# A memory tile multiplied ahead of the modulation: its load, its norm and its two halves moved to the program's first instructions

## The chip, the cores and the metric

The kernel runs on one core of one Trainium2 chip. A time is the device time of one execution in microseconds (us). Three executions of the kernel before gave 1676.72, 1678.35 and 1678.55 us, median 1678.35. One more execution was profiled; all rows below are from it. Engines: PE multiplies matrices, DVE, ACT and POOL do the element-wise work, and SP's queue issues nearly all of the transfers.

## The reference, cut to what matters

256 tokens of width 1024 go through two blocks. The first mixes the tokens (attention with 8 heads, mLSTM with 4) and then sends them through 32 experts; the second is a GLA layer and an S5 layer, which both attend to a memory of 256 rows.

```python
mod = jax.nn.silu(c) @ w_ada[l] + b_ada[l]                 # 6 x 1024 numbers: the modulation
sh1, sc1, g1, sh2, sc2, g2 = jnp.split(mod, 6, axis=-1)
h = modulate(x, norm1_g[l], sh1, sc1)                      # rms_norm(x) * (1 + sc1) + sh1
proj = h @ w_in[l]
# ... attention, mLSTM, w_out, router, experts ...
mem_n = rms_norm_2(mem, mem_norm_w)                        # second block, but it needs only mem
k, v = jnp.split(mem_n @ w_kv, 2, axis=-1)                 # w_kv[0]: 1024 x 2048
```

The product `mem_n @ w_kv[0]` depends on nothing that the first block computes. The kernel therefore places its four tiles among the first block's work.

## The kernel before, in words

All arithmetic is float32. The weights come as tiles of 2 MB (128 partitions x 4096 numbers, which is 1024 rows by 512 columns). They go through a ring of three slots, in the order that the tuple `FRONT` gives; tile n goes to slot n modulo 3, and its load waits until PE has finished tile n-3. `tile(n)` in SP's program does this: it waits on `tile_done` and issues the load.

The names of tiles: A0 to A11 are the modulation (`w_ada`). `ada_tile` (L278) multiplies one of them by the vector silu(c), which is short work: 16 instructions of PE. ACT copies the result (`take_part`, L565), and then `ada_columns` (L290, piece C) or `ada_row` (L300, piece G) turns it into the layout wanted, and DVE adds the bias. A0 to A3 give shift and scale of the first norm, without which the input of all further multiplications, `hT`, cannot be made. Q, K, V, U0, U1, VM, OM are `w_in`, O0 and O1 are `w_out`, and M0 to M3 are the four quarters of `w_kv[0]`: M0 and M1 make the keys `kmT`, M2 and M3 the values `vm`. A tile of `w_in` or of `w_kv` is multiplied in two halves (`half_tile`, L259 for kind "tm", L264 for kind "fm"; M00 is the first half of M0).

Stage `stage_mix` begins the program. Its order is written out by hand, engine by engine, and semaphores join the engines. PE does A0, C0, A1, C1, A2, the transposes of the scaled x (`turn`, L186), C2, A3, C3. DVE then makes `hT` (L701), PE the gates (L408), and Q, K, V and the rest follow without a break. The memory is loaded behind tile Q (L381). Its squares on ACT (L590), its scaling on DVE (L751), its transposes on PE (`turn` between K0 and K1) and its multiplication by the norm's weights on DVE (L754, result `memT`) lie beside Q, K and V. M00 and M01 stand beside the mLSTM's steps, between A7 and A8.

`stage_route` follows. PE does M1 (L972), transposes the normed x, does A10, M20, the router's logits (L983), G10, transposes back (L989), M21, A11, M30, the five ranking multiplications (L996 to L1000), G11 and M31. Beside them DVE picks the experts: it finishes `chosen` (L1093), which the ranking waits for, and after the ranking it makes `rank`, the last third of `h2` (L1127) and the last row of the modulation (L1041). SP loads A10, M2, the first expert's six half tiles, A11, M3, one row, and the second expert's six half tiles as the ring's slots come free. A stage ends when every engine is done, and `stage_experts` begins.

PE's results of pieces go to two banks in turn. The string given to `TwoBanks` names the pieces in order and the engine that empties each; a piece waits until the piece two places before it has been taken.

## Time and profile before

| | |
|---|---|
| three executions, median | 1678.35 us |
| the profiled execution | 1676.78 us |
| its span, first to last instruction | 1675.0 us |
| PE busy in the span | 1566.1 us, 93% |
| mean granted clock of PE | 0.982 of full |
| start of PE's first multiplication | 12.53 us |
| start of the gates' multiplications | 36.81 us |
| start of the first Q half | 41.92 us |
| `stage_route`, PE's first to last instruction | 228.4 to 284.8 us |
| first instruction of `stage_experts` on DVE | 287.18 us |

The share of PE over the whole span says that PE is nearly always at work. It does not say where it is not: the gaps lie in the first 37 us, at the ends of stages and in a few waits later. The change touches the first 37 us, two halves in the middle of `stage_mix`, and the end of `stage_route`. So the profile is read there: which wait ends last before each step of PE.

In a row of the timeline the first number is the start, the second the time that the group spans, then engine, line, operation, result and operands, count, and in brackets the idle time before it and what ended it. One multiplication in the program is two instructions in the trace (x16 for the 8 of an `ada_tile`, x32 for the 16 of an "fm" half).

### The profile page before, as it was taken

How to read it: one execution, taken by the hardware profiler on the slowest of the kernel's cores; microseconds unless marked ns; L12 is line 12 of the kernel's file. 1: busy time of each engine (PE TensorE's matmuls, PEld its weight loads, DVE VectorE, ACT ScalarE, POOL GpSimd, SP SyncE). 2: the span in 40 equal slices, each digit the busy share in tenths (PEclk: the TensorE clock that was granted, in tenths of full speed). 3: DMA queues.
4: the chain of work that ended last, by engine and by line, in shares of the span. 5: the costliest groups of instructions: out<-in, count | busy, mean ns of one | idle time of the engine just before them, and what ended most of it. 6: DMA issues, size and time to landing. Idle time of an engine off the chain costs nothing. (4 is left out here: it accounts for less than half of the span.)

```text
span 1675.0 us, 20622 instructions
## 1 busy us (share of the span) xinstructions
PE 1566.1 (93%) x8428; PEld 917.0 (55%) x8428; DVE 578.7 (35%) x958; ACT 321.9 (19%) x547; POOL 54.0 (3%) x125
## 2 busy tenths in 40 slices
PE   5999998999999999994999999988999899699997
PEld 2485654444344444442445887547777775388843
DVE  2445323111111111113202111215999999720000
ACT  2222101111111111111200201003333343230000
POOL 0000000000000000000000000001111111000000
PEclk8999999999999999997999999998999999799999
DMA  9444647899999999993232242342333333124330
GB/s 402 169 157 188 257 200 318 339 422 422 422 422 422 422 422 422 422 410 130 107 144 101 101 151 101 146 156 94 146 114 113 115 148 129 63 101 151 151 151 25
DMA packets 46024, 371.59 MB, mean 222 GB/s; under 512 B 5888, under 2 KB 10368, under 8 KB 11408
## 3 DMA queue, kind: packets, MB, share of 16 engines
q1 hardware_dynamic: 45824, 369.75, 55.0%
q10 hardware_dynamic: 144, 1.05, 0.2%
q8 instruction: 40, 0.66, 0.2%
q14 instruction: 16, 0.13, 0.0%
HBM read 369.73 MB, written 1.05 MB: 221 GB/s over the span
## 5 line engine op out<-in xcount | busy, mean ns | idle before, releaser
L1228 PE MATMUL ps<-ring,x_gathered 128*64 128x512 f32 x1024 | 225.2, 592 | 0.9 <-DVE x_gathered L1296 0.9
L1911 PE MATMUL ps<-hT,ring 128*128 128x256 f32 x768 | 174.7, 386 | 1.9 <-PEq L113 1.9
L1416 PE MATMUL ps<-ring,zT 128*128 128x512 f32 x384 | 165.5, 592 | 0.0
L1911 PEld LDWEIGHTS ps<-hT,ring 128*128 128x128 f32 x768 | 146.0, 192 | 29.9 <-issue 10.4
L1228 PEld LDWEIGHTS ps<-ring,x_gathered 128*64 128x64 f32 x1024 | 73.6, 137 | 146.6 <-issue 146.6
L1305 DVE TENSOR_TENSOR act_slots<-gate,ps 64x512 f32<-64x512 f32 x32 | 22.1, 690 | 378.6 <-ACT gate L1267 378.6
L1416 PEld LDWEIGHTS ps<-ring,zT 128*128 128x128 f32 x384 | 72.9, 190 | 90.1 <-issue 89.9
L1251 PE MATMUL ps<-ring,act_turned 128*64 128x512 f32 x512 | 116.9, 598 | 0.0
L1529 PE MATMUL ps<-hT,ring 128*128 128x256 f32 x512 | 111.9, 380 | 0.0
L2086 PE MATMUL ps<-uT,ring 128*128 128x256 f32 x512 | 111.0, 379 | 0.0
L1529 PEld LDWEIGHTS ps<-hT,ring 128*128 128x128 f32 x512 | 96.8, 190 | 16.0 <-issue 3.1
L2086 PEld LDWEIGHTS ps<-uT,ring 128*128 128x128 f32 x512 | 97.2, 190 | 13.2
L1524 PE MATMUL ps<-ring,hT 128*128 128x512 f32 x192 | 83.7, 594 | 2.4 <-PEq L113 2.4
L1203 PE MATMUL ps<-y,selT 64*128 64x512 f32 x272 | 77.9, 641 | 4.2 <-DVEq L1290 3.5
L1251 PEld LDWEIGHTS ps<-ring,act_turned 128*64 128x64 f32 x512 | 33.9, 136 | 79.1 <-issue 54.8
L259 PE MATMUL ps<-ring,hT 128*128 128x512 f32 x160 | 69.8, 593 | 0.0
L1192 PEld LDWEIGHTS ps<-sel,h 128*128 128x128 bf16 x1584 | 48.7, 99 | 27.5 <-issue 27.5
L1524 PEld LDWEIGHTS ps<-ring,hT 128*128 128x128 f32 x192 | 36.0, 190 | 47.0 <-issue 47.0
L1267 ACT ACTIVATE gate<-ps 64x512 f32<-64x512 f32 x32 | 18.9, 591 | 188.1 <-PE ps L1228 188.1
L1192 PE MATMUL ps<-sel,h 128*128 128x64 bf16 x1584 | 52.6, 194 | 0.0
L259 PEld LDWEIGHTS ps<-ring,hT 128*128 128x128 f32 x160 | 29.9, 190 | 35.8 <-issue 35.8
L1934 PE MATMUL ps<-s_x_re,c_bar 128*32 128x256 f32 x128 | 11.1, 418 | 38.4 <-issue 35.4
(446 smaller groups left out, 1676.9 us busy)
## 6 DMA issues: line engine op xcount, KB each, us to landing
ring<-in_experts SPq DMA_DIRECT2D x192, 1024.0 KB, 15.8
ring<-in_weights SPq DMA_DIRECT2D x75, 2048.0 KB, 7.5
b_raw<-in_s_b SPq DMA_DIRECT2D x16, 128.0 KB, 7.4
c_raw<-in_s_c SPq DMA_DIRECT2D x16, 128.0 KB, 7.2
x<-in_x ACTq DMA_DIRECT2D x1, 1024.0 KB, 5.3
mix_room<-in_mem SPq DMA_DIRECT2D x1, 1024.0 KB, 17.2
rows_b_g<-in_rows SPq DMA_DIRECT2D x1, 1024.0 KB, 19.3
out<-x SPq DMA_DIRECT2D x2, 512.0 KB, 2.7
```

The costliest lines, as they stand in the source:

```text
L259: last = pe.matmul(bank, src[:, kk, h * P:(h + 1) * P], w[:, kk, :], start=(kk == 0), stop=(kk == KD - 1))
L1192: last = pe.matmul(xg_ps[:, f, :], a["h2"][:, t, part, f * P:(f + 1) * P], sel[:, t, :], start=(t == 0 and part == 0), stop=(t == TT - 1 a ...
L1203: last = pe.matmul(acc[:, t, n, :], selT[rows, b, t * P:(t + 1) * P], y[rows, :], start=start, stop=stop, skip_group_check=True)
L1228: last = pe.matmul(h_ps[rows, :], xg[:, f, :], w[:, kk, m, :], start=(f == 0), stop=(f == KD - 1))
L1251: last = pe.matmul(y_ps[rows, :], act_t[:, f, :], w[:, kk, n * 512:(n + 1) * 512], start=(f == 0), stop=(f == 3))
L1267: act.activation(gate[:], h_ps[lower, :], ACT.Silu).then_inc(silu_done, 1)
L1305: dve.tensor_tensor(act_s[:], gate[:], h_ps[upper, :], ALU.mult).then_inc(act_ready, 1)
L1416: last = pe.matmul(self.bank(n, t), self.zT[:, 8 * kb + kk, t * P:(t + 1) * P], w[:, kk, :], start=(first and kk == 0), stop=(self.ends(i) ...
L1524: last = pe.matmul(bank, k.hT[:, kk, h * P:(h + 1) * P], w[:, kk, :], start=(kk == 0), stop=(kk == KD - 1))
L1529: last = pe.matmul(bank[:, f, :], w[:, kk, (2 * h + f) * P:(2 * h + f + 1) * P], k.hT[:, kk, :], start=(kk == 0), stop=(kk == KD - 1))
L1911: last = pe.matmul(out[:, f, :], w[:, kk, (2 * h + f) * P:(2 * h + f + 1) * P], rhs[:, kk, :], start=(kk == 0), stop=(kk == KD - 1))
L2086: last = pe.matmul(o[:, f, :], w[:, kk, f * P:(f + 1) * P], uT[:, 8 * r + kk, :], start=(r == 0 and kk == 0 and f % 2 == 0), stop=(r == 1 ...
```

## The change

The tile M0 leaves `FRONT` and stands as one more tile at the end of the weights (index `T_END`). The memory and this tile are now loaded ahead of the ring's first three tiles; the tile goes in two halves to two buffers, `qk` and `mix`, that are not yet in use. ACT squares the memory before x, DVE scales the memory before x, and PE begins with the memory's transposes. DVE then makes `memT`, PE multiplies M00, then A0, then M01, and goes on with C0 as before. In the middle of the stage, where M00 and M01 were, M20 and M21 stand now, as kind "tm", with their results to `vm`. In `stage_route` M3 takes the places that M2 had, and the two places of M3 (beside A11 and after the ranking) are gone, with one load of 2 MB less.

```diff
-FRONT = (..., "A6", "A7", "M0", "A8", "A9",
-         "O0", "O1", "M1", "A10", "M2", "A11", "M3")
+FRONT = (..., "A6", "A7", "M2", "A8", "A9",
+         "O0", "O1", "M1", "A10", "M3", "A11")
...
@@ stage_mix, sync
                 sp.dma_start(k.const[:], d["consts"]).then_inc(small_in, 16)
+                sp.dma_start(mem, d["mem"]).then_inc(mem_in, 16)
+                for i in range(2):
+                    sp.dma_start(first_w[i], d["weights"][T_END][:, i * 2048:(i + 1) * 2048]).then_inc(first_in, 16)
                 for n in range(RING):
                     tile(n)
...
                 tile(4)
-                sp.dma_start(mem, d["mem"]).then_inc(mem_in, 16)
...
@@ stage_mix, tensor
+                def first_half(h):
+                    p = f"M0{h}"
+                    out = banks.bank(p).rearrange("p (f t) -> p f t", f=2)
+                    for f in range(2):
+                        for kk in range(KD):
+                            w = first_w[kk // 4].rearrange("p (k n) -> p k n", k=4)[:, kk % 4, (2 * h + f) * P:(2 * h + f + 1) * P]
+                            last = pe.matmul(out[:, f, :], w, k.memT[:, kk, :], start=(kk == 0), stop=(kk == KD - 1))
+                    last.then_inc(banks.done(p), 1)
+                pe.wait_ge(mem_scaled, TT)
+                turn(k, pe, memn, KD, fm(0, 4), mem_turned)
+                pe.wait_ge(memT_ready, 1)
+                pe.wait_ge(first_in, 32)
+                first_half(0)
                 pe.wait_ge(crep_ready, 1)
-                for m in range(3):
-                    ada_tile(k, banks, pe, m, crep)
-                    if m < 2:
-                        ada_columns(k, banks, pe, m, part)
+                ada_tile(k, banks, pe, 0, crep)
+                pe.wait_ge(*banks.free("M01"))
+                first_half(1)
+                ada_columns(k, banks, pe, 0, part)
+                ada_tile(k, banks, pe, 1, crep)
+                ada_columns(k, banks, pe, 1, part)
+                ada_tile(k, banks, pe, 2, crep)
...
                 half("K0")
-                pe.wait_ge(mem_scaled, TT)
-                turn(k, pe, memn, KD, fm(0, 4), mem_turned)
                 half("K1")
...
-                half("M00", "fm", k.memT)
+                half("M20", "tm", k.memT)
...
-                half("M01", "fm", k.memT)
+                half("M21", "tm", k.memT)
...
@@ stage_mix, scalar: the memory's squares stand before x's
-                for m in range(4):
+                take_fm("M00", a["kmT"][:, 0:2, :])
+                take_part(0)
+                take_fm("M01", a["kmT"][:, 2:4, :])
+                for m in range(1, 4):
                     take_part(m)
...
@@ stage_mix, vector
                 dve.tensor_copy(crep[:], bc(csil[:], 2, 32)).then_inc(crep_ready, 1)
+                dve.wait_ge(mem_rstd_ready, 1)
+                for t in range(TT):
+                    dve.tensor_scalar(memn[:, t, :], mem[:, t, :], rstd_m[:, t:t + 1], None, ALU.mult).then_inc(mem_scaled, 1)
+                ...
+                dve.wait_ge(mem_turned, KD)
+                for f in range(KD):
+                    last = dve.tensor_scalar(k.memT[:, f, :], fm(0, 4)[:, f, :], k.col("mem_norm_w", f), None, ALU.mult)
+                last.then_inc(memT_ready, 1)
                 take_columns(0, 0)
...
@@ stage_route, tensor
-                half_tile(k, banks, pe, "M20", "tm", k.memT)
+                half_tile(k, banks, pe, "M30", "tm", k.memT)
...
-                half_tile(k, banks, pe, "M21", "tm", k.memT)
+                half_tile(k, banks, pe, "M31", "tm", k.memT)
                 ada_tile(k, banks, pe, 11, a["crep"])
-                half_tile(k, banks, pe, "M30", "tm", k.memT)
                 pe.wait_ge(chosen_ready, 1)
...
                 ada_row(k, banks, pe, 11, a["part"])
-                half_tile(k, banks, pe, "M31", "tm", k.memT)
```

PE's order at the program's start, before (L278 is an A tile, L290 a C piece, L186 the transposes of x, L408 the gates):

```order
L278 MATMUL ps<-ring,crep 32x512 x8
L290 MATMUL ps<-const,ada_part 128x1 x4
L278 MATMUL ps<-ring,crep 32x512 x8
L290 MATMUL ps<-const,ada_part 128x1 x4
L278 MATMUL ps<-ring,crep 32x512 x8
L186 MATMUL ps<-const,mix_room 128x128 x16
L290 MATMUL ps<-const,ada_part 128x1 x4
L278 MATMUL ps<-ring,crep 32x512 x8
L290 MATMUL ps<-const,ada_part 128x1 x4
L408 MATMUL ps<-hT,w_gate 4x256 x16
```

The same place in the changed kernel (the first L186 transposes the memory, L405 is M00 and, after the first A tile, M01):

```order
L186 MATMUL ps<-const,mix_room 128x128 x16
L405 MATMUL ps<-memT,qk 128x256 x4
L405 MATMUL ps<-memT,mix 128x256 x4
L405 MATMUL ps<-memT,qk 128x256 x4
L405 MATMUL ps<-memT,mix 128x256 x4
L278 MATMUL ps<-ring,crep 32x512 x8
L405 MATMUL ps<-memT,qk 128x256 x4
L405 MATMUL ps<-memT,mix 128x256 x4
L405 MATMUL ps<-memT,qk 128x256 x4
L405 MATMUL ps<-memT,mix 128x256 x4
L290 MATMUL ps<-const,ada_part 128x1 x4
L278 MATMUL ps<-ring,crep 32x512 x8
```

The memory's transposes and one half stand ahead of the first A tile, the other half behind it; from the C piece on the order is the old one.

PE at the end of `stage_route`, before (L259 are the halves, L278 is A11, L996 and the four below it the ranking, L300 G11):

```order
L259 MATMUL ps<-ring,memT 128x512 x8
L278 MATMUL ps<-ring,crep 32x512 x8
L259 MATMUL ps<-ring,memT 128x512 x8
L996 MATMUL ps<-chosen,const 128x32
L997 MATMUL ps<-chosen,const 128x32
L998 MATMUL ps<-chosen,const 128x32
L999 MATMUL ps<-chosen,const 128x32
L1000 MATMUL ps<-chosen,const 128x32
L300 MATMUL ps<-ada_part,const 128x512
L259 MATMUL ps<-ring,memT 128x512 x8
```

And the same place in the changed kernel:

```order
L259 MATMUL ps<-ring,memT 128x512 x8
L278 MATMUL ps<-ring,crep 32x512 x8
L1017 MATMUL ps<-chosen,const 128x32
L1018 MATMUL ps<-chosen,const 128x32
L1019 MATMUL ps<-chosen,const 128x32
L1020 MATMUL ps<-chosen,const 128x32
L1021 MATMUL ps<-chosen,const 128x32
L300 MATMUL ps<-ada_part,const 128x512
```

The half between A11 and the ranking and the half behind G11 are gone.

## Rows read from the trace of the kernel before

**Rows 1.** The page, part 1: busy time, share of the span, instructions.
```profile
PE 1566.1 (93%) x8428; PEld 917.0 (55%) x8428; DVE 578.7 (35%) x958; ACT 321.9 (19%) x547; POOL 54.0 (3%) x125
```

**Rows 2.** Stretches: length, busy (instructions) of PE, PEld, DVE, ACT, POOL, clock, DMA share, GB/s.
```profile
12.50:36.80 24.30, 16.82 (x112) 8.15 (x112) 8.39 (x28) 5.36 (x8) 0.00 (x0) 0.86 1.01 425
...
41.90:194.60 152.70, 152.59 (x692) 95.89 (x690) 69.30 (x141) 36.02 (x78) 4.33 (x5) 1.00 0.47 184
```

**Rows 3.** SP's timeline: issue of the ring's first three tiles; their time to landing.
```profile
1.64 1.68 SPq L370 DMA_DIRECT2D ring<-in_weights  x3
...
DMA to landing us min/median/max: 10.8/15.2/19.4
```

**Rows 4.** Timeline of the first 60 us, all engines.
```profile
7.65 1.04 ACT L572 ACTIVATE mix_room<-x 128x1024 f32<-128x1024 f32 x1
...
10.24 0.71 POOL L179 TENSOR_TENSOR x_rstd<-x_rstd,const 128x2 f32<-128x2 f32 x1
...
12.53 3.64 PE L278 MATMUL ps<-ring,crep 128*32 128x512 f32 x16 [12.53 <-DMA ring<-in_weights]
...
18.05 1.41 DVE L681 TENSOR_SCALAR mix_room<-x,x_rstd 128x1024 f32<-128x1024 f32 x2
...
20.51 1.05 PE L290 MATMUL ps<-const,ada_part 128*128 128x1 f32 x8 [0.72 <-ACT ada_part L565]
...
28.81 1.92 PE L278 MATMUL ps<-ring,crep 128*32 128x512 f32 x16 [0.32 <-DMA ring<-in_weights]
...
31.45 1.05 PE L290 MATMUL ps<-const,ada_part 128*128 128x1 f32 x8 [0.72 <-ACT ada_part L565]
...
33.04 3.71 DVE L701 TENSOR_SCALAR hT<-ps,mod 128x256 f32<-128x256 f32 x8
...
36.81 5.19 PE L408 MATMUL ps<-hT,w_gate 128*4 128x256 f32 x32 [4.30 <-DVE hT L701]
...
41.92 18.29 PE L259 MATMUL ps<-ring,hT 128*128 128x512 f32 x42
```

**Rows 5.** Stretches of 1 us in the gates' multiplications, columns as in rows 2.
```profile
37.00:38.00 1.00, 1.00 (x6) 0.28 (x4) 0.00 (x0) 0.00 (x0) 0.00 (x0) 0.50 0.96 410
...
40.00:41.00 1.00, 1.00 (x12) 0.40 (x10) 0.00 (x0) 0.00 (x0) 0.00 (x0) 0.99 1.00 426
```

**Rows 6.** PE's timeline later in `stage_mix`.
```profile
62.63 1.91 PE L186 MATMUL ps<-const,mix_room 128*128 128x128 f32 x16
...
168.57 1.92 PE L278 MATMUL ps<-ring,crep 128*32 128x512 f32 x16
170.42 7.17 PE L264 MATMUL ps<-memT,ring 128*128 128x256 f32 x32
```

**Rows 7.** Timelines of PE, then DVE and ACT, at the end of `stage_route`.
```profile
266.08 1.92 PE L278 MATMUL ps<-ring,crep 128*32 128x512 f32 x16
268.83 7.13 PE L259 MATMUL ps<-ring,memT 128*128 128x512 f32 x16 [0.83 <-DMA ring<-in_weights]
...
277.78 7.03 PE L259 MATMUL ps<-ring,memT 128*128 128x512 f32 x16
...
261.82 0.23 DVE L1093 TENSOR_TENSOR chosen<-is_first,is_second 128x64 f32<-128x64 f32 x1
...
277.04 0.23 DVE L1114 SCALAR_TENSOR_TENSOR rank<-ps,chosen 128x64 f32<-128x64 f32 x1 [10.28 <-PE ps L1000]
...
280.42 0.68 DVE L1041 TENSOR_TENSOR rows_b_g<-ps,rows_b_g 128x512 f32<-128x512 f32 x1
287.18 0.48 DVE L1288 MEMSET y<- 128x512 f32 x1 [6.08 <-issue]
...
284.84 0.60 ACT L1016 ACTIVATE vm<-ps 128x512 f32<-128x512 f32 x1 [8.24 <-PE ps L259]
```

**Rows 8.** SP's timeline and time to landing: A11 and M3; then A11 alone.
```profile
242.47 3.96 SPq L947 DMA_DIRECT2D ring<-in_weights  x2
...
DMA to landing us min/median/max: 21.4/21.4/21.4
```

More of the change, by code:

```diff
@@ L329, in stage_mix @@
         memn, mem = tokens(r3), tokens(r4)
+        first_w = [x[:].rearrange("p t n -> p (t n)") for x in (qk, mix)]
         scores, pT = (r[:].rearrange("p (b h t q) -> p b h t q", b=2, h=2, t=TT) for r in (r3, r4))
@@ L336, in stage_mix @@
         ig, fg = gate_rows[:, 0, :], gate_rows[:, 1, :]
-        banks = TwoBanks(k, "mix", "A0:act C0:dve A1:act C1:dve A2:act C2:dve A3:act C3:dve GT:dve Q0:act Q1:act K0:act K1:act "
+        banks = TwoBanks(k, "mix", "M00:act A0:act M01:act C0:dve A1:act C1:dve A2:act C2:dve A3:act C3:dve GT:dve Q0:act Q1:act K0:act K1:act "
                          "V0:act V1:act U00:act U01:act U10:act A4:act U11:act G4:dve VM0:act A5:act VM1:act G5:dve "
-                         "OM0:act OM1:act A6:act C6:dve A7:act M00:act C7:dve M01:act A8:act C8:dve A9:act C9:dve")
-        names = ("small_in", "mix_const_in", "pos_in", "rows_in", "x_in", "mem_in", "w_gate_in", "cexp_ready", "crep_ready",
+                         "OM0:act OM1:act A6:act C6:dve A7:act M20:act C7:dve M21:act A8:act C8:dve A9:act C9:dve")
+        names = ("small_in", "first_tile_in", "mix_const_in", "pos_in", "rows_in", "x_in", "mem_in", "w_gate_in", "cexp_ready", "crep_ready",
                  "x_summed", "x_rstd_ready", "x_scaled", "x_turned", "hT_ready",
@@ L587, in _ @@
                 act.activation(q4[96:100, 0:P], b[:, 0:P], ACT.Exp, bias=sc[:, 2:3]).then_inc(e_ready, 1)
-                act.wait_ge(mem_in, 16)
-                for t in range(TT):
-                    act.activation(memn[:, t, :], mem[:, t, :], ACT.Square, accum_out=ss_m[:, t:t + 1]).then_inc(mem_summed, 1)
                 take("Q1", qk[:, 1, 0:512])
@@ L637, in _ @@
                 take_part(7)
-                take_fm("M00", a["kmT"][:, 0:2, :])
-                take_fm("M01", a["kmT"][:, 2:4, :])
+                take("M20", a["vm"][:, 0, 0:512])
+                take("M21", a["vm"][:, 1, 0:512])
                 take_part(8)
@@ L677, in _ @@
                 dve.tensor_copy(crep[:], bc(csil[:], 2, 32)).then_inc(crep_ready, 1)
-                take_columns(0, 0)
+                dve.wait_ge(mem_rstd_ready, 1)
+                for t in range(TT):
+                    dve.tensor_scalar(memn[:, t, :], mem[:, t, :], rstd_m[:, t:t + 1], None, ALU.mult).then_inc(mem_scaled, 1)
                 dve.wait_ge(x_rstd_ready, 1)
@@ L747, in _ @@
                 dve.tensor_copy(q4[0:4, :], b).then_inc(m_ready, 1)
-                dve.wait_ge(mem_rstd_ready, 1)
-                for t in range(TT):
-                    dve.tensor_scalar(memn[:, t, :], mem[:, t, :], rstd_m[:, t:t + 1], None, ALU.mult).then_inc(mem_scaled, 1)
-                dve.wait_ge(mem_turned, KD)
-                for f in range(KD):
-                    last = dve.tensor_scalar(k.memT[:, f, :], fm(0, 4)[:, f, :], k.col("mem_norm_w", f), None, ALU.mult)
-                last.then_inc(memT_ready, 1)
                 dve.wait_ge(quads_ready, 1)
@@ L936, in stage_route @@
         tps = k.ps[:, 0:4, :].rearrange("p b (f t) -> p (b f) t", f=2)
-        banks = TwoBanks(k, "route", "M10:act M11:act A10:act M20:act G10:dve M21:act A11:act M30:act G11:dve M31:act")
+        banks = TwoBanks(k, "route", "M10:act M11:act A10:act M30:act G10:dve M31:act A11:act G11:dve")
         names = ("router_in", "norm_f_in", "x1_summed", "x1_rstd_ready", "x1_scaled", "x1_turned", "h_ready", "logits_done",
@@ L952, in _ @@
                 tile(TILE_OF["A10"])
-                tile(TILE_OF["M2"])
+                tile(TILE_OF["M3"])
                 for j in range(RING):
@@ L956, in _ @@
                 tile(TILE_OF["A11"])
-                tile(TILE_OF["M3"])
                 at = ROWS["norm_f_g"][0]
@@ L1022, in _ @@
                 take("A10", a["part"][:])
-                take("M20", a["vm"][:, 0, 0:512])
+                take("M30", a["vm"][:, 0, 512:1024])
                 act.wait_ge(h_turned, 1)
@@ L1028, in _ @@
                 act.activation(dl[:], dl[:], ACT.Exp).then_inc(exp_done, 1)
-                take("M21", a["vm"][:, 1, 0:512])
+                take("M31", a["vm"][:, 1, 512:1024])
                 act.wait_ge(rest_ready, 1)
@@ L1033, in _ @@
                 take("A11", a["part"][:])
-                take("M30", a["vm"][:, 0, 512:1024])
-                take("M31", a["vm"][:, 1, 512:1024])
             @block.vector
@@ L2298 @@
         wide(g["s5_w_in_2"][0]), kv[1], wide(g["s5_w_glu_2"][0]),
-        in_order(wide(g["w_out_2"][1]), "s5"),
+        in_order(wide(g["w_out_2"][1]), "s5"), front["M0"][None],
     ]
@@ L2302 @@
     weights = np.concatenate(groups, axis=0)
[L2303 removed]
+    assert weights.shape[0] == T_END + 1
     def by_feature(v, n):
```

13 lines of the change are left out of this document (7 added, 6 removed).

## The prediction

> **What bounds the kernel now.** I read the shares of busy time first, then the timeline around each place that the change touches, then the transfers there. PE is busy for 93% of the span [rows 1], so work on PE that is removed is worth its time, and so is work that moves into a gap. After the first Q half PE does not stop for the rest of `stage_mix`: 152.59 of 152.70 us [rows 2]. There every microsecond of work is a microsecond of time. The first 37 us are different. From 12.5 to 36.8 us PE is busy for 16.82 of 24.30 us while the transfers run at 425 GB/s with a share of 1.01 [rows 2]: the queue is full, and PE waits for tiles (the bracket of the row at 28.81 names the DMA) [rows 4]. In `stage_route` the end is set by PE's last half at 277.78 and ACT's copy of it, which ends at 284.84 + 0.60 = 285.44; DVE is done at 280.42 + 0.68 = 281.1 [rows 7].
>
> So the question is one of two places: what the front of the program pays for M0, and what the router's end gives back. The middle is an exchange.
>
> **The front, step by step.** The change puts 3 MB (memory 1 MB, tile 2 MB) ahead of A0, and 16 transposes, 7 us of multiplication and a DVE step ahead of A0 on PE.
>
> First the transfers. The ring's first three tiles are issued from 1.64 us on, the third at about 2.8, and land 10.8 to 19.4 us after issue, so at 12.4 and 22.2 us: 4.9 us for each 2 MB [rows 3]. A0's own 4.9 us begin at 7.5. The memory, in that place now, lands after 2.45 us, at 10.0; M0 at 14.9; A0, A1 and A2 7.35 us later than before, at about 19.8, 24.7 and 29.6.
>
> Now PE's chain, which starts with the memory:
> - ACT squares the memory from 10.0 on. For x the squares began at 7.65 and POOL's rstd ended at 10.24 + 0.71 = 10.95, together 3.30 us [rows 4]. That gives 13.3.
> - DVE scales two halves: 1.41 us [rows 4], 14.75.
> - PE's 16 transposes take 1.91 us at full clock [rows 6]. PE has done nothing before. Before the change its first tile, A0, took 3.64 us where later ones take 1.92, a factor of 1.9 [rows 4, 6]. So 3.6 us: 18.4.
> - DVE makes `memT` from PSUM by 8 instructions like those of `hT`: 3.71 us plus 0.05 [rows 4], 22.15. PE stands still meanwhile; x's squares and scaling (another 3.3 + 1.4 us behind the memory's) fit in.
> - M00 takes 7.0 us from its start to the next piece's at full clock (7.17 with its end) [rows 6]. [...] Some 3.3 to 3.6 us at half speed lose 1.7 to 1.8 us; I take 1.9, because the work before the pause is short. 31.05.
> - A0 1.9 (landed since 19.8) and M01 7.0: 39.95. C0 0.9: 40.85. ACT's copies of M00, of A0's result and of M01 (0.60 each) lie beside PE's next piece.
> - A1 1.9, then 0.72 of waiting for ACT's copy [rows 4], C1 0.95, A2 1.9: 46.3. No wait for a tile any more.
> - x's transposes 1.8, C2 0.9, A3 1.9: 50.9. A3's load is issued when A0 is done (32.9) into an empty queue; even with the 19.4 us of rows 3, which were those of a full one, it would come at 52.3, and with their shortest, 10.8, at 43.7, before PE wants it at 49.0. K, V and Q follow A1, A2, A3 in the same way; Q is issued at 42.8 and wanted at 62.
> - From A3's end to the gates' start: 36.81 - 30.73 = 6.1 us, the copy, C3, DVE's column and `hT` [rows 4]. The gates start at 57.0.
>
> Before, they started at 36.81 [rows 4]. The front grows by 20.2 us. The transfers alone would have moved it by 7.35. The difference is the step that decides: once PE's chain begins at 14.75, it has 42 us of work and hand-offs in a row, and it is later than every tile. The gap that M0 was to fill was not there at the time at which `memT` can be there.
>
> [...]
>
> **The middle.** The memory's transposes between K0 and K1 go: 1.91 us with its end, 1.8 from start to start [rows 6]. DVE loses the scaling and `memT` there and ACT two squares, on engines that PE does not wait for. M20 and M21 replace M00 and M01: a "tm" half takes 7.03 us, an "fm" half 7.17 [rows 6, 7], so -0.1 at most. Their copies are of equal size, and the load stands in the same place of the ring.
>
> **The router's end.** M30 and M31 take the places of M20 and M21, at equal cost. Two halves go from PE. A11 runs at 266.08 as before, since its load is at the same place of the queue: issued at 242.47, landed at 263.9 [rows 8]. It ends at 268.0. `chosen` has been ready since 262.05 [rows 7], so the ranking follows at once. It took from 275.9 (268.83 + 7.0) to DVE's start at 277.04, so 1.15 us: DVE starts at 269.15. DVE then needs 281.1 - 277.04 = 4.06 us: 273.2. G11 needs ACT's copy of A11, at about 269.1 behind the copy of `h2`, and is done at 270.2, in DVE's shadow. The stage now ends with DVE at 273.2, not with ACT at 285.44: -12.2 us. The two halves are worth 14.06 and the 0.83 us wait for M3's load goes too [rows 7], but DVE's tail, once covered by M31, is 3 us long behind PE and now stands free. SP's wait for the last row and the second expert's loads are earlier than this, with 2 MB less in the queue.
>
> The experts, GLA and S5 are unchanged but for the tiles' slots in the ring.
>
> **The sum.** +20.2 - 1.8 - 0.1 - 12.2 = +6.1 us. Against the profiled execution, 1676.8, that is 1682.9; this execution lay 1.6 us below the median of the three, and against that median it is 1684.4. I say 1684.
>
> **The bounds of what no row shows.** [...] The memory's transposes: at full clock -1.7. The memory's landing: at the earliest 9.5, or 2.5 us later if its packets share the queue with M0's. The clock of the later short pieces: A1 to A3 could lose up to 1.7 us once, as A0 did. The experts' start: PE stands still for some 6 us where it was 3.5, and may lose up to 1.7 us more, or nothing. Together 1680.7 to 1691, most of it in 1681.5 to 1687.5.
>
> **The rivals.** A measurement of this kernel tells 0.2% (3.4 us) from no change, so "same" is 1675.0 to 1681.7.
>
> 1. Faster: the transfers set the front, as now. Then only 7.35 us are added there and the total is 1678.35 + 7.35 - 1.8 - 0.1 - 12.2 = 1671.6. For it: the queue's share of 1.01 and PE's 7.5 idle us of 24.3 [rows 2]. Against it: those idle us are spread over hand-offs of 0.7 us and waits between tiles, and M00 cannot start before `memT`, at 22.15, where A0 lands at 19.8. The point from which it decides: the front may grow by 14.1 us at most; my chain would have to be 6 us too long. 9%.
> 2. No change that can be measured: PE runs at full clock in the memory's transposes and M00, -3.6, so 1680.8, and some hand-off is shorter. 13%.
> 3. [...] 10%.
> 4. The router's end gives less: A11's load shares the queue with the second expert's first load, which is now issued when A10 is done (about 246) and not at 266, and lands as late as M3 did, 268.8. Then A11 is 2.7 us later and the total 1687.1. Against it: A11 is issued first. 8%.
>
> My forecast has 60%. It and rivals 3 and 4 are slower by over 0.2%: 78%. Same 13%, faster 9%. The range has to leave out no more than 2 in 10: from 1678 (rival 1 out, rival 2 in) to 1689 (rival 3's end out).
>
> **What would show each step.** The gates' first multiplication starts near 57 us, and its shift from 36.81 is the front's cost; M00 starts near 22 behind DVE's `memT` and takes 8 to 9.5 us; A1, A2, A3 start without a wait for a DMA; the first Q half starts near 62. The end of `stage_route`, from M1's first multiplication to DVE's first instruction of the experts, is 58.8 us before (228.38 to 287.18) and should be 46.6. I am wrong if PE waits for the ring's tiles in the front, if M00 starts before 20 us, or if the router's stage gives back 14 us or more.

## The result, and the profile after

The changed kernel takes 1687.74 us (median of 7 runs, 1685.55 to 1691.43); the kernel before took 1680.97 us in the 7 runs beside it (1676.72 to 1683.32). The ratio is 1.0044, with a 95% interval from 1.0029 to 1.0058: slower by 0.3 to 0.6%. The forecast was 1684.0 us in a range of 1678 to 1689, slower with a chance of 78%. Against the median that it started from (1678.35) it was a growth of 5.7 us; measured was one of 6.8. The starting point had been low, though: in these runs the kernel before lies 2.6 us above 1678.35, so the growth was forecast within 1.1 us and the absolute time only within 3.7, near the top of the range.

The profiled execution of the changed kernel was its slowest: 1691.43 us with a span of 1689.7, against 1676.78 and 1675.0. These 14.7 us are more than the medians differ, so a second profile of the same kernel was taken (e1 below, span 1683.4). Where the two disagree, both are told.

The page's first part. PE's busy time grew by 10.7 us [rows 1], although the number of its instructions did not: 8428 in both.

```profile
PE 1576.8 (93%) x8428; PEld 925.1 (55%) x8428; DVE 578.7 (34%) x958; ACT 321.7 (19%) x547; POOL 54.4 (3%) x125
```

The timeline of the front, PE's rows with the DVE and ACT rows that release them:

```profile
10.00 1.06 ACT L592 ACTIVATE mix_room<-mix_room 128x1024 f32<-128x1024 f32 x1 [2.29 <-DMA mix_room<-in_mem]
...
14.83 3.68 PE L186 MATMUL ps<-const,mix_room 128*128 128x128 f32 x16 [14.83 <-DVE mix_room L703]
...
18.54 3.23 DVE L709 TENSOR_SCALAR memT<-ps,cols 128x256 f32<-128x256 f32 x8 [1.43 <-PE ps L186]
...
21.82 3.78 PE L405 MATMUL ps<-memT,qk 128*128 128x256 f32 x8 [3.32 <-DVE memT L709]
...
25.40 2.77 PE L405 MATMUL ps<-memT,mix 128*128 128x256 f32 x8
...
28.01 1.89 PE L405 MATMUL ps<-memT,qk 128*128 128x256 f32 x8
...
31.55 1.92 PE L278 MATMUL ps<-ring,crep 128*32 128x512 f32 x16
...
41.36 1.92 PE L278 MATMUL ps<-ring,crep 128*32 128x512 f32 x16
...
44.98 1.92 PE L278 MATMUL ps<-ring,crep 128*32 128x512 f32 x16
...
49.51 1.92 PE L278 MATMUL ps<-ring,crep 128*32 128x512 f32 x16
52.15 1.05 PE L290 MATMUL ps<-const,ada_part 128*128 128x1 f32 x8 [0.72 <-ACT ada_part L585]
57.50 5.48 PE L431 MATMUL ps<-hT,w_gate 128*4 128x256 f32 x32 [4.30 <-DVE hT L731]
```

The chain runs as it was written down beforehand: memory at 10.0, transposes from 14.8, `memT`, M00 at 21.8, A0, M01, the other modulation tiles. The four rows of L278 are A0 to A3, and none has a DMA in its bracket; before, A3's had one, of 0.32 us [rows 4]. PE no longer waits for tiles in the front, it is itself late. The clock shows in durations: the same 16 transposes took 1.91 us in the old place [rows 6] and take 3.68 here; M00's four quarters (8 instructions each) take 3.78, 2.77, 1.89 and 1.89. The views' own clock column says 1.00 for the whole of this trace from 12 to 54 us, also in the row below, where PE had only 5 instructions; in e1's row of the same stretch, where the column says 0.50, it had 6. So the front is read by durations here:

```profile
22.00:24.00 2.00, 2.00 (x5) 1.64 (x6) 0.00 (x0) 0.00 (x0) 0.00 (x0) 1.00 1.02 434
```

The gates start at 57.50, 20.7 us later than before [rows 4].

The end of `stage_route`, PE's rows, then DVE's, which answer to rows 7:

```profile
273.34 4.13 PE L1005 MATMUL ps<-w_router,hT 128*128 128x36 f32 x32
277.27 2.05 PE L300 MATMUL ps<-ada_part,const 128*128 128x512 f32 x2
279.12 3.62 PE L1011 MATMUL ps<-const,hT 128*128 128x128 f32 x16
282.53 7.36 PE L259 MATMUL ps<-ring,memT 128*128 128x512 f32 x16
289.81 1.92 PE L278 MATMUL ps<-ring,crep 128*32 128x512 f32 x16
...
292.58 0.39 PE L1021 MATMUL ps<-chosen,const 128*128 128x32 f32 x2
```
```profile
293.01 0.23 DVE L1132 SCALAR_TENSOR_TENSOR rank<-ps,chosen 128x64 f32<-128x64 f32 x1 [4.13 <-PE ps L1021]
...
296.39 0.68 DVE L1059 TENSOR_TENSOR rows_b_g<-ps,rows_b_g 128x512 f32<-128x512 f32 x1
298.44 0.48 DVE L1306 MEMSET y<- 128x512 f32 x1 [1.38 <-issue]
```

The last row, DVE's first instruction of the experts, came at 287.18 before and comes at 298.44. Between A11's multiplications and the ranking there is no half any more, and DVE's row with `rows_b_g` is now the last thing the stage waits for. But the router's own pieces are slow here. The stretches (columns as in rows 2) name the reason:

```profile
276.00:278.00 2.00, 2.00 (x10) 1.75 (x10) 0.41 (x2) 0.00 (x0) 0.00 (x0) 0.59 1.06 442
278.00:280.00 2.00, 2.00 (x7) 1.11 (x6) 1.65 (x13) 0.00 (x0) 0.00 (x0) 0.50 1.05 434
280.00:282.00 2.00, 2.00 (x11) 2.00 (x10) 1.54 (x13) 0.00 (x0) 0.00 (x0) 0.50 0.97 412
282.00:284.00 2.00, 2.00 (x7) 1.25 (x6) 1.43 (x6) 1.23 (x1) 0.00 (x0) 0.71 0.96 395
```

PE was busy all through, 2.00 of 2.00 us in each row, and the clock fell late in the 36-column multiplications (L1005), which start at 273.34 and take 4.13 us: it is 1.00 from 275 to 276 us and 0.67 from 276 to 277. In the profile shown of before, where the same multiplications start at 252.94 and take 3.66 us, it is 1.00 from 250 to 264 us.

The forecast had named no third place, but there is one: the first 16 instructions of the GLA multiplications, behind the experts' end. They took 7.11 us before. PE's row in the changed kernel, and a stretch in it:

```profile
794.28 8.80 PE L1542 MATMUL ps<-ring,hT 128*128 128x512 f32 x16 [2.38 <-PEq L113]
```
```profile
796.00:798.00 2.00, 2.00 (x4) 0.85 (x3) 0.00 (x0) 0.00 (x0) 0.00 (x0) 0.50 0.77 256
```

### The profile page after: what moved, and what is told of

It reads as the page before. It is cut to its first block and busy times, and to the rows that moved or that the text cites. A ratio compares the mean times of both kernels' runs of the same rounds, so it can differ in the third digit from the quotient of the medians.

```text
span 1689.7 us, 20622 instructions
## 1 busy us (share of the span) xinstructions
PE 1576.8 (93%) x8428; PEld 925.1 (55%) x8428; DVE 578.7 (34%) x958; ACT 321.7 (19%) x547; POOL 54.4 (3%) x125
## 5 line engine op out<-in xcount | busy, mean ns | idle before, releaser
L259 PE MATMUL ps<-ring,hT 128*128 128x512 f32 x160 | 69.6, 593 | 0.0
L259 PEld LDWEIGHTS ps<-ring,hT 128*128 128x128 f32 x160 | 30.0, 190 | 36.3 <-issue 36.3
L1448 DVE TENSOR_TENSOR x<-x,ps 128x512 f32<-128x512 f32 x8 | 5.5, 687 | 120.0 <-PE ps L1434 120.0
## 6 DMA issues: line engine op xcount, KB each, us to landing
mix<-in_weights SPq DMA_DIRECT2D x1, 1024.0 KB, 12.2
```

The lines of the kernel that those rows point to most:

```text
L259: last = pe.matmul(bank, src[:, kk, h * P:(h + 1) * P], w[:, kk, :], start=(kk == 0), stop=(kk == KD - 1))
```

## The experiments

Each kernel's ratio is to the kernel before, run beside it. Five marks, in us, are read from each trace: the start of the gates' multiplications; PE's start on M1 (the M tile in its old place behind O1); the time from there to DVE's first instruction of the experts ("router"); from there to ACT's copy of the last expert's gate ("experts"); and from there to the end of the span ("tail"). M1 and the last three add up to the span.

| kernel | median us (runs) | ratio, 95% | gates | M1 | router | experts | tail |
|---|---|---|---|---|---|---|---|
| before | 1680.97 (7) | | 36.81 | 228.38 | 58.80 | 461.3 | 926.6 |
| changed | 1687.74 (7) | 1.0044, 1.0029 to 1.0058 | 57.50 | 248.78 | 49.66 | 461.6 | 929.6 |
| e1 changed, again | 1685.88 (6) | 1.0037, 1.0023 to 1.0050 | 56.03 | 245.60 | 48.01 | 461.1 | 928.7 |
| e2 without M0 | 1672.22 (5) | 0.9952, 0.9937 to 0.9967 | 36.86 | 228.22 | 46.33 | 462.6 | 930.9 |
| e3 without the tile's load | 1686.39 (5) | 1.0041, 1.0025 to 1.0057 | 56.55 | 246.27 | 48.00 | 461.2 | 928.8 |
| e4 loads alone | 1686.28 (9) | 1.0038, 1.0023 to 1.0053 | 44.37 | 236.59 | 58.66 | 461.2 | 927.2 |
| e5 filled, too long | 1689.70 (6) | 1.0046, 1.0028 to 1.0063 | 58.38 | 249.24 | 46.32 | 462.4 | 930.6 |
| e6 A0 in the first pause | 1684.73 (12) | 1.0022, 1.0011 to 1.0033 | 52.87 | 243.94 | 46.33 | 462.5 | 930.6 |
| e7 M0 in the pause for `hT` | 1680.82 (12) | 1.0002, 0.9989 to 1.0015 | 54.34 | 245.41 | 46.32 | 461.3 | 928.8 |
| e8 that, ranking first | 1677.22 (12) | 0.9973, 0.9961 to 0.9984 | 50.07 | 239.48 | 46.33 | 461.3 | 929.8 |
| e9 before, again | 1676.8 (1) | | 36.88 | 228.45 | 58.66 | 461.2 | 926.7 |
| e10 before, again | 1678.95 (1) | | 36.85 | 229.68 | 59.57 | 461.2 | 926.7 |
| e11 filled, fitting | 1683.17 (12) | 1.0018, 1.0008 to 1.0029 | 53.33 | 244.66 | 46.32 | 462.5 | 930.7 |
| e12 e8 with the old slots | 1675.22 (7) | 0.9967, 0.9955 to 0.9980 | 50.50 | 239.95 | 44.67 | 462.2 | 926.6 |

### e1: the changed kernel again

No edit.

> The changed kernel once more, for a second profile and a second set of times. Theory: the front's cost is a chain on PE that the order fixes, so the gates start at 57.5 us again (within 0.5) and the ratio to before is near 1.0044. The first profile also had 3 us at the low clock between the router's logits and the second M3 half (276 to 283 us). If that stretch belongs to the change, it is there again and M1's start to the experts' first DVE instruction takes 49.7 us. If it was chance, that stretch takes 46.6 us.

The ratio came out as in the first comparison. In this profile the same steps are shorter: transposes 3.40, M00 8.6 us, and the low stretch beside the router costs 1.7 us and not 3.3 (48.01 and 49.66 against the 46.33 us of kernels without one). PE's rows of M00's first two quarters:

```profile
21.46 3.51 PE L405 MATMUL ps<-memT,qk 128*128 128x256 f32 x8 [3.32 <-DVE memT L709]
24.80 1.89 PE L405 MATMUL ps<-memT,mix 128*128 128x256 f32 x8
```

And the clock in it, in the front and beside the router:

```profile
22.00:24.00 2.00, 2.00 (x6) 1.59 (x5) 0.00 (x0) 0.00 (x0) 0.00 (x0) 0.50 1.08 459
24.00:26.00 2.00, 2.00 (x9) 1.69 (x9) 0.00 (x0) 0.00 (x0) 0.00 (x0) 0.86 1.00 426
...
274.00:276.00 2.00, 2.00 (x5) 0.86 (x5) 1.63 (x13) 0.00 (x0) 0.00 (x0) 0.50 1.04 438
276.00:278.00 2.00, 2.00 (x15) 2.00 (x14) 1.56 (x13) 0.00 (x0) 0.00 (x0) 0.71 1.03 434
```

So a single profile of one kernel is not good to better than some 6 us; the stretches at low clock are not equally long in both.

The front differs in one more thing. The transposes took 3.40 us here and not 3.68, because the clock rose before their end: the last two start 0.11 us apart, the first ones 0.21, and an instruction takes 0.27 us at the end and 0.42 before. So, by these durations, the clock rose when PE had done 3 us of transposes and nothing else, and fell again in the pause behind them (0.50 in the row of 22 to 24 us). In the first profile it had not risen by then.

### e2: M0 left out, nothing ahead of A0

```diff
-                sp.dma_start(mem, d["mem"]).then_inc(mem_in, 16)
-                for i in range(2):
-                    sp.dma_start(first_w[i], d["weights"][T_END][:, i * 2048:(i + 1) * 2048]).then_inc(first_in, 16)
...
-                first_half(0)
...
-                first_half(1)
```

The memory's load, norm and transposes are back in their old places.

> The changed kernel with M0 left out altogether: memory loaded, normed and transposed where it was before, no early tile, kmT's first half set to zero (so the keys of half the memory heads are not computed), M2 in the middle and the short router's end kept. Theory: the router's end is worth 12.2 us and the exchange in the middle 0.1, so 12.3 us faster than before (ratio 0.9927) and 19 to 20 us faster than the changed kernel. Rival: the two removed halves are worth their full 14.1 us plus the 0.8 us wait for M3, ratio 0.991. Second rival: the low clock beside the router eats 3 us, ratio 0.9945.

The router's stage took 46.33 us, which puts its gain at 12.5 us. The time, though, did not fall by as much as expected: 0.9952 and not 0.9927. The experts took 462.6 us, 1.3 more than before, and the tail 930.9, 4.3 more. That is where the rest went: the span is 7.0 us shorter. The first is the low clock at the experts' start (0.50 from 272 to 280 us), which the prediction had among its bounds; the second is the first sign that the tail is not untouched.

### e3: the tile's load left out, its multiplications kept

```diff
-        first_w = [x[:].rearrange("p t n -> p (t n)") for x in (qk, mix)]
+        first_w = [x.rearrange("p t n -> p (t n)") for x in (mem, mem)]
...
-                for i in range(2):
-                    sp.dma_start(first_w[i], d["weights"][T_END][:, i * 2048:(i + 1) * 2048]).then_inc(first_in, 16)
```

> The changed kernel without the early load of M0's 2 MB: M00 and M01 are multiplied from the memory's own numbers in its place (the keys of half the memory heads are wrong numbers). All ring tiles land 4.9 us earlier. Theory: PE's chain sets the front, so the gates start at 57.5 us as in the changed kernel and the ratio to before stays 1.0044. Rival: the early loads set the front, then the gates start 4.9 us earlier, at 52.6, and the ratio is 1.0015.

With 2 MB less ahead of A0 the gates start at 56.55, inside the 56.03 to 57.50 of the two profiles with the load, and the ratio is 1.0041 beside 1.0037 and 1.0044, which the intervals do not tell apart. The transfers do not set the changed kernel's front.

### e4: the loads alone

The kernel before, with memory and M0's tile loaded ahead of A0, the tile never used.

```diff
+                sp.dma_start(mem, d["mem"]).then_inc(mem_in, 16)
+                for i in range(2):
+                    sp.dma_start(first_w[i], d["weights"][TILE_OF["M0"]][:, i * 2048:(i + 1) * 2048]).then_inc(first_in, 16)
                 for n in range(RING):
```

> The kernel before with nothing but the two early loads (memory and M0's tile, 3 MB, ahead of A0); M0 stays in the ring and the early copy is not used. All work is where it was. Theory: the front of the kernel before is set by its loads, so everything there moves by 7.35 us: A0 at 19.8, gates at 44.2, and the whole by 7.35 us, ratio 1.0044. Rival: PE's pauses take some of it up, gates before 42 and ratio under 1.003.

PE's rows of A2, A3 and the gates (the view ends within the gates' row; all 32 take 5.58 us):

```profile
29.85 1.92 PE L278 MATMUL ps<-ring,crep 128*32 128x512 f32 x16 [0.69 <-DMA ring<-in_weights]
...
36.38 1.92 PE L278 MATMUL ps<-ring,crep 128*32 128x512 f32 x16 [1.93 <-DMA ring<-in_weights]
...
44.37 1.88 PE L411 MATMUL ps<-hT,w_gate 128*4 128x256 f32 x8 [4.30 <-DVE hT L705]
```

The same 3 MB move this kernel's gates by 7.6 us (7.35 had been worked out), and here the brackets name the DMA. With e3: the front of before is set by the transfers, the changed one by PE's chain.

### e5 and e11: PE kept busy ahead of the transposes and of M00

Needless multiplications before the transposes and behind them: 9 and 7 in e5, 4 and 3 in e11.

```diff
+                pe.wait_ge(small_in, 32)
+                idle_work(4)
                 pe.wait_ge(mem_scaled, TT)
                 turn(k, pe, memn, KD, fm(0, 4), mem_turned)
+                idle_work(3)
                 pe.wait_ge(memT_ready, 1)
```

> The changed kernel with needless multiplications on PE (128x512, into an unused bank): 9 from the constants' landing at 7.5 us to the memory's transposes, 7 in the pause in which DVE makes memT. They delay nothing by more than 0.5 us and keep PE's clock up. Theory: 3.6 to 4.4 us of the front are the low clock in the transposes (3.4 to 3.7 us where 1.9 is full speed) and in M00 (8.7 to 10.3 where 7.0 is), so the gates start at 52.5 to 53.5 and the ratio to before is 1.0015 to 1.002. Rival: the clock is low there for another reason than the pauses, the gates stay at 56 to 57.5 and the ratio at 1.0037 or above.

> As e5, with 4 needless multiplications ahead of the memory's transposes and 3 in the pause for memT, which fit (one takes 0.87 us at full clock and 1.7 us at the low one). Theory: the low clock in the transposes and in M00 costs 3 to 4.5 us of the front, so the gates start at 53 to 54.5 and the ratio to before is 1.0015 to 1.0025. Rival: the filling does not raise the clock in time, the gates stay at 56 or later and the ratio at 1.0035.

In e5 the filling overran: its first 9 ran to 17.8 us and held the transposes up by 2.9 us, its last 7 held M00 up to 25.43. Its time says nothing for either theory, but the transposes took 1.91 us. e11 fits, as PE's rows show:

```profile
7.49 5.65 PE L411 MATMUL ps<-const 128*128 128x512 f32 x8 [7.49 <-DMA const<-in_consts]
14.79 1.97 PE L186 MATMUL ps<-const,mix_room 128*128 128x128 f32 x16 [1.65 <-DVE mix_room L711]
16.59 2.74 PE L411 MATMUL ps<-const 128*128 128x512 f32 x6
20.27 1.99 PE L405 MATMUL ps<-memT,qk 128*128 128x256 f32 x8 [0.93 <-DVE memT L717]
...
53.33 6.52 PE L439 MATMUL ps<-hT,w_gate 128*4 128x256 f32 x32 [4.30 <-DVE hT L739]
```

Transposes and M00 run at full clock; M00 ends at 27.4 and not at 30.1 to 31.6, the gates start 2.7 to 4.2 us earlier than in the two profiles of the changed kernel. The gates' multiplications take 6.52 us here, against 4.92 and 5.48, so a part may be lost again at once (e10, below, shows 6.31 in the kernel before). The ratio is 1.0018. The low clock in transposes and M00 costs 3 to 4 us of front, and even without it the change is slower.

### e6: A0 ahead of M00, in the pause for `memT`

```diff
                 turn(k, pe, memn, KD, fm(0, 4), mem_turned)
+                pe.wait_ge(crep_ready, 1)
+                ada_tile(k, banks, pe, 0, crep)
                 pe.wait_ge(memT_ready, 1)
...
-                ada_tile(k, banks, pe, 0, crep)
+                ada_columns(k, banks, pe, 0, part)
```

> The changed kernel with A0 between the memory's transposes and M00, in PE's pause for memT; M00, C0, M01 follow. A0 lands at 19.8 us. Theory: PE's chain sets the front, so filling 2 to 3 us of the pause brings the gates forward by 1.5 to 3 us, to about 54.5, ratio 1.002 to 1.003. Rival: A0 at the low clock takes 3.6 us and pushes M00 behind memT; nothing is gained, gates at 56.5 or later.

```profile
14.75 3.28 PE L186 MATMUL ps<-const,mix_room 128*128 128x128 f32 x16 [14.75 <-DVE mix_room L703]
19.90 1.92 PE L278 MATMUL ps<-ring,crep 128*32 128x512 f32 x16 [1.88 <-DMA ring<-in_weights]
21.76 1.99 PE L405 MATMUL ps<-memT,qk 128*128 128x256 f32 x8
...
52.87 3.58 PE L431 MATMUL ps<-hT,w_gate 128*4 128x256 f32 x16 [4.30 <-DVE hT L731]
```

PE's rows (the last is cut off by the view's end; all 32 take 6.35 us): A0 lands at 19.90 (19.8 had been worked out) and fits ahead of M00 without moving it. M00 then runs at full clock (1.99 us for its first quarter, and not 3.78 or 3.51): the pause is shorter, 1.88 us and not 3.3. The gates come 3.2 to 4.6 us earlier than in the changed kernel; the ratio is 1.0022.

### e7: M0 in the pause for `hT`

M0's load behind A3's, its halves between C3 and the gates.

```diff
                 tile(3)
+                for i in range(2):
+                    sp.dma_start(first_w[i], d["weights"][T_END][:, i * 2048:(i + 1) * 2048]).then_inc(first_in, 16)
...
                 ada_columns(k, banks, pe, 3, part)
+                pe.wait_ge(first_in, 32)
+                for h in range(2):
+                    pe.wait_ge(*banks.free(f"M0{h}"))
+                    first_half(h)
                 pe.wait_ge(hT_ready, 1)
```

> The changed kernel with M00 and M01 between C3 and the gates, where PE has a pause of 4.3 us for hT, and M0's 2 MB loaded behind A3; memory's load, norm and transposes stay early. Theory: the front then costs 2.5 us (memory ahead of A0), 1.1 us (M00 waits for its tile, at 36.2), 14 us less the pause of 4.3, less 1.7 us because the gates no longer start at the low clock: the first Q half starts at 53.7 and not at 62, the whole is 9 us faster than the changed kernel and 2.3 us faster than before, ratio 0.9986. Rival: a multiplication costs its 14 us wherever it stands in the front, then the first Q half starts at 58 or later and the ratio is 1.001 or above.

The pause of 4.30 us for `hT`, which all kernels above keep, is filled, and the ratio falls from 1.0037 to 1.0002. It is less than expected, for the reason that PE's rows show: another pause of 2.48 us, for M0's own load, and its low clock (0.50 from 38 to 42 us). M00 starts 1.1 us later than expected (37.28 and not 36.2), and the two halves take 17.1 us, 3.1 more than 14.

```profile
37.28 3.78 PE L405 MATMUL ps<-memT,qk 128*128 128x256 f32 x8 [2.48 <-DMA mix<-in_weights]
40.85 3.19 PE L405 MATMUL ps<-memT,mix 128*128 128x256 f32 x8
...
54.34 3.62 PE L431 MATMUL ps<-hT,w_gate 128*4 128x256 f32 x32
57.89 27.73 PE L259 MATMUL ps<-ring,hT 128*128 128x512 f32 x64
```

The first Q half starts at 57.89, where 53.7 was expected. A second stretch of low clock (0.50 from 212 to 214 us), behind a wait of 2.46 us for tile O0 that ended at 211 us, cost another 1.7 us, and the tail was 2.3 us longer than before.

### e8: the tile in two halves, and the ranking ahead of A11

M0 is packed by halves of its columns and each half has its own load and semaphore, so M00 waits for 1 MB only; and PE's five ranking pieces stand ahead of A11, so that DVE's 4 us lie beside A11 and G11.

```diff
-                pe.wait_ge(first_in, 32)
                 for h in range(2):
+                    pe.wait_ge((first_in, second_in)[h], 16)
...
-                ada_tile(k, banks, pe, 11, a["crep"])
                 pe.wait_ge(chosen_ready, 1)
...
                 pe.matmul(k.ps[:, 5, 0:32], k.c("ones"), chosen[:, 1, :], start=False, stop=True).then_inc(ranked, 1)
+                ada_tile(k, banks, pe, 11, a["crep"])
```

> As the kernel before it in this list, and two things more: M0 is packed by halves of its columns, so that M00 needs only the first 1 MB and starts at C3's end (gain 1.1 us), and in the router's stage the five ranking multiplications stand ahead of A11, so that DVE's tail begins 1.9 us earlier and the stage ends at ACT's and G11's pace (gain 1.6 us). Theory: ratio 0.9970, the first Q half at 52.6, M1 to the experts' first DVE instruction 44.7 us. Rival: the router's tail is bound by the copy of h2 on ACT and nothing is gained there, 46.3 us, ratio 0.998.

```profile
31.16 3.31 PE L278 MATMUL ps<-ring,crep 128*32 128x512 f32 x16 [1.17 <-DMA ring<-in_weights]
35.17 1.05 PE L290 MATMUL ps<-const,ada_part 128*128 128x1 f32 x8 [0.70 <-ACT ada_part L585]
36.08 7.15 PE L405 MATMUL ps<-memT,qk 128*128 128x256 f32 x32
43.07 7.07 PE L405 MATMUL ps<-memT,mix 128*128 128x256 f32 x32
50.07 3.62 PE L431 MATMUL ps<-hT,w_gate 128*4 128x256 f32 x32
```

From C3 on PE does not stop, and the gates start 4.3 us earlier than in e7. This version is faster than the kernel before: 0.9973, from 0.9961 to 0.9984. The first Q half comes at 53.63 (52.6 was expected). Its router took 46.33 us with a low clock in it (0.77, 0.50 and 0.88 in the stretches of 2 us from 266 to 272; 44.7 us was expected), e12's 44.67 without (1.00 from 262 to 270), so the ranking's place is worth 1.7 us.

### e9 and e10: the kernel before, twice more

No edit.

> The kernel before once more, for its trace. In the first profile of it the time from the last expert's gate copy to the end is 926.6 us, and the first GLA half takes 7.1 us. In the profiles of kernels with the short router's end it is 928.7 to 930.9, and that half 8.8 to 9.8 us with a low clock. Theory: that is the phase of the clock, which differs from run to run, so here the tail is longer than 926.6, up to 931. Rival: the tail belongs to the change (tiles in other slots of the ring), and is 926.6 to 927.2 here.

> The same once more, for the same question: by the theory the tail lies anywhere from 926.6 to 931, by the rival within 0.6 of 926.9.

Both tails are as in the first profile: 926.7 and 926.7. In e10 the clock fell beside the router in this kernel too (0.84, 0.50 and 0.80 in the stretches of 2 us from 256 to 262, all 1.00 in e9): M1 to the experts took 59.57 us, 0.9 more than in e9. So the low stretch there is not the change's own doing. The gates' multiplications took 6.31 us in e10 and 5.19 in the first profile, with nothing changed.

### e12: e8 with one needless tile behind A11

The tile makes no work but takes a slot, so that all later tiles of the ring lie and are loaded as in the kernel before.

```diff
-         "O0", "O1", "M1", "A10", "M3", "A11")
+         "O0", "O1", "M1", "A10", "M3", "A11", "X")
...
                 tile(TILE_OF["A11"])
+                tile(TILE_OF["X"])
...
+                k.wait_tile(pe, TILE_OF["X"])
+                pe.sem_inc(k.tile_done, 1)
```

> e8 with one needless tile of 2 MB loaded behind A11 in the router's stage and not multiplied, so that every later tile stands in the same slot of the ring as before the change, and the second expert's loads wait as long. From the last expert's gate copy to the end the kernel before takes 926.6 to 926.7 us in three profiles (926.6, 926.6, 926.7) and 927.2 with the early loads alone; e8 takes 929.8, the other kernels with the short router's end 928.7 to 930.9. Theory A: the ring's slots or the loads' order behind them cause it, then the tail is near 926.7 here, and the ratio to before 0.995 to 0.996. Theory B: it is where the steps fall against the clock's changes, which the length of the work ahead decides; then the tail is 928.7 or more and the ratio near 0.9975.

The tail is 926.6 us, the number of the kernel before to a tenth, and PE's row of the first GLA multiplications is back at its old length:

```profile
781.07 7.11 PE L1544 MATMUL ps<-ring,hT 128*128 128x512 f32 x16 [2.37 <-PEq L113]
```

2 MB more are moved, and the span is 3.4 us shorter than e8's (1673.5 against 1676.9): router 1.7 and tail 3.2 us less, experts 0.9 and the part ahead of M1 0.5 more. By the times it is the fastest of those that compute everything, 0.9967, but its interval overlaps that of e8, so that its lead over e8 rests on the two profiles. Against the kernel before it is faster.

## Why the prediction was right, step by step

**The front.** The step that decided was that PE's chain, not the transfers, sets the gates' start. It held: 57.0 us forecast, 57.50 and 56.03 in two profiles, no DMA ahead of A1 to A3. e3 and e4 show it from both sides: without the tile's load the front stays, with the loads alone it moves by 7.6 us. Rival 1 (the transfers set the front) falls with e3.

The single steps up to M00's end were off by at most 0.8 us: the memory's landing 10.0 (10.0), the transposes 14.83 (14.75) for 3.68 and 3.40 (3.6), M00's start 21.82 and 21.46 (22.15; DVE's `memT` took 3.2 and not 3.7 us), M00 9.7 and 8.6 (8.9). That transposes and M00 would run at low clock was taken from A0's 3.64 us and the gates' row [rows 4, 5], and it came out so; e6 and e11 show that the idle time ahead does it, since with PE busier the same pieces take 1.97 us (e11) and 7.0 (both). The 1.9 us that the sum has for M00's low clock are the author's estimate, and no run shows that number: rows 5 have 0.50 at 37 us and 0.99 at 40 behind the pause of 4.30 us, and M00 lost 2.7 us in the first profile, 1.6 in e1 and 1.8 in e3 against its 7.0. In e1 and e6 the clock rose while PE had done nothing but transposes (3.40 and 3.28 us for the 16, against 3.68). Rival 2 (full clock) gives 1680.8 on those terms, 1.0015 of the median it started from, and e11, which makes that case, measured 1.0018. That they agree is in part luck, for e11's ratio also holds a longer gates' row and a tail 4.1 us longer, which the rival's sum does not have. Rival 3 (a clock that stays low through all of M00, +5.1 us, to 1689.5) did not happen, and no run shows its 5.1 us, which is also in the range's upper end: in both profiles M00's second half is at full clock, 1.89 us for each of its quarters. The sum left one thing out: O0's wait for its tile, 1.09 us before, is 2.33 in one profile and 1.18 in the other.

**The middle.** The shift of PE is 21.0 us at the first Q half and 19.25 us behind the place where the memory's transposes stood, so these give 1.75 (1.8). M20 and M21 take 7.13 and 7.03 us.

**The router.** Forecast was 46.6 us for the stage and a gain of 12.2. Without a low clock it took 46.32 or 46.33 us in e2, e5, e6, e7 and e11; A11 did not land late (rival 4): neither profile has a wait of 0.2 us or more on PE between M1's start and the end of its work in the stage. In the two profiles of the changed kernel the stage took 49.66 and 48.01, since the clock fell beside the router (0.50 from 278 to 282 us and from 274 to 276). The bounds had named such a stretch for the experts' start, not for here. It came there as well: in e2, e5, e6 and e11, whose router was free of it and whose clock then was 0.50 from 272 to 280, 294 to 302, 288 to 296 and 288 to 298 us, the experts took 462.4 to 462.6 us and not 461.3. The stage's gain through to the experts' end is therefore 8.8 and 11.0 us in the two profiles of the changed kernel, 11.2 to 11.3 in these four and 12.5 in e7.

**The tail: the step that failed.** The prediction says that experts, GLA and S5 "are unchanged but for the tiles' slots in the ring" and gives these slots nothing. With the slots shifted the tail is 2 to 4 us longer, and e12, which puts them back, has the old tail. In the five profiles with the old slots (before, e4, e9, e10, e12) the tail is 926.6 to 927.2 us; in the nine with one tile less in the ring (the changed kernel, e1 to e3, e5 to e8, e11) it is 928.7 to 930.9. It is no wait for a tile: from the last gate copy to the first GLA multiplication every profile has 34.2 us. In the changed kernel 1.7 of the 3.0 us lie in the first 16 instructions of the GLA stage, at 0.50 instead of full clock. That part, 1.7 us or 2.6 to 2.7, is in all nine profiles with the shifted slots (8.80 or 9.70 to 9.79 us for the 16) and in none of the five others (7.10 or 7.11). The remaining 0.5 to 1.6 us lie behind them, where these traces have more low clock than the first one (the changed kernel 0.93 from 1110 to 1210 us and 0.80 from 1435 to 1485, the kernel before 0.95 and, from 1425 to 1475, 0.83); of that e4, with the old slots, has 0.6 us too (0.95 and, from 1430 to 1480, 0.80).

**The sum.** In e1: front and middle up to M1 +17.2 (forecast +18.3), router -10.8 (-12.2), experts -0.2 (0), tail +2.1 (0), together +8.3 (+6.1). In the first profile: +20.4, -9.1, +0.4 and +3.0, together +14.7. Both are set against one profile of the kernel before that was among its fastest executions; by medians the growth is 6.8 us in one comparison and 5.6 in the other. So the total owes something to luck. The clock beside the router and the longer tail cost 3.5 us that the sum did not have in e1 and 6.1 in the first profile; against them stands a front that was 1.1 us cheaper in e1, but 2.1 dearer in the first profile.

**What stays open.** Why the clock is low in the first GLA multiplications when the slots are shifted is not settled. Their loads are issued elsewhere relative to the experts' end (3.5 us ahead of the last gate copy in the changed kernel, at it before), but PE's pause ahead of them is 2.4 us in both and the transfers' share 1.7 to 3.7 us behind their start is 0.77 in both. What does differ is the stretch from 20 to 10 us ahead of these multiplications, in which PE stands still. The kernel before, then the changed one:

```profile
762.66:772.66 10.00, 0.00 (x0) 0.00 (x0) 5.66 (x4) 3.04 (x5) 0.89 (x2) 0.55 0.47 202
774.28:784.28 10.00, 0.00 (x0) 0.00 (x0) 5.67 (x4) 3.03 (x5) 0.89 (x2) 0.52 0.02 8
```

With the old slots the GLA tiles are still being loaded there (a share of 0.46 to 0.48 in all five), with the shifted ones hardly anything is (0.02 to 0.13 in all nine). Whether that does it is not shown. The rival that e12 was to exclude, that it only matters where the steps fall against the clock's changes, is weakened but not gone: the low stretch, at 0.50, begins 18.7 us ahead of these multiplications both in e4 and in e5, and ends 1.6 us ahead of them in e4, with the old slots, but 5.2 us behind their start in e5; yet in all five profiles with the old slots it begins 18.7 to 19.0 us ahead, while in the others it is anywhere from 18.7 to 22.0. e12 changes the loads beside the router too, and it is one profile. Nor is it shown what decides between a full and a low clock beside the router: both were seen in the kernel before and in changed ones.

## What to carry to other kernels

Work moved into a stretch in which an engine waits for transfers fills it only if its own operands are there by then: follow the operand's chain (landing, norm, transposes, copy out of PSUM) before counting the idle time, for here 7.5 us of idle time stood against a chain of 22 us ahead of the first multiplication. The same piece of work paid off in the pause behind that chain (e7, e8), where its operands had long been ready and where it also spared the next piece a start at low clock (the gates' row took 3.62 us there, 5.48 and 4.92 in the changed kernel). When a shared ring gets one tile more or less, look at the stages behind it as well, and test with a needless tile. And add the stages up: a stretch of low clock that spares one stage (the router in e2, 46.33 us) can stand in the next (its experts, 462.6 us for 461.3).

## What the runs showed of the hardware that was not expected

- The low clock may not go away by filling one pause. In e11 the transposes and M00 were at full clock (4.3 us less than in the changed kernel's profile), and the gates' multiplications then took 6.52 us behind the same 4.30 us pause, against 5.48. This is a hint and no proof, since the same row took 6.31 us in e10. Without any pause ahead (e7, e8) it took 3.62.
- The clock fell to 0.50 while PE was busy all the time: beside the router in the changed kernel, late in 4.13 us of 36-column multiplications, it cost 3.3 us in one profile, 1.7 in the next, and nothing in e2, e5, e6, e7 and e11. e3, e8 and e10 show it at the same place.
- A pause of 1.88 us ahead of A0 in e6 left it at full clock; one of 1.17 us ahead of A3 in e8 did not (3.31 us for 1.92, the clock 0.50 from 32 to 34 us), one of 2.48 us in e7 did not (0.50 from 38 to 42). In these three the length of the pause alone does not decide.
- M0's load, put behind A3's in a full queue (a share of 0.92 to 1.08 from 28 to 37 us), held M00 up till 37.28 us (e7); its first half alone, with its own semaphore, no longer did: M00 started at 36.08 behind C3 without a wait (e8), where A3 had taken 1.4 us longer at low clock.
- The clock rose with nothing but transposes done: in e1 when PE had done 3 us of them and nothing before (the instructions took 0.42 us and then 0.27), in e6 likewise (3.28 us for the 16, against 3.68 where it did not rise).
